# The sample's expert keys moved out of the projection stage into the mixer stage before it

## What is computed

```python
h = rmsnorm(x, norm_mix)
z = h @ w_in                                  # 1024 -> 5888 columns, for all rows
oa = windowed attention; ob = retention       # mixers A and B
x = x + (sigmoid(ga) * (oa @ w_branch_a) + sigmoid(gb) * (ob @ w_branch_b)) @ w_out
h2 = rmsnorm(x, norm_ffn)
q = h2 @ w_q                                  # 1024 -> 2048, 8 heads of 2 x 128
s1, s2 = q halves times 128 sub keys each
top 16 of s1, of s2, then of the 256 sums     # 128 experts for each row
y = sum_k gate_k * gelu(h2 . expert_u[k]) * expert_v[k]
out = rmsnorm(x + y, norm_final)
```

## Time and profile before

| | us |
|---|---|
| median of 3 runs | 4076.27 |
| profiled execution | 4112.39 |
| its span | 4110.5 |
| projection stage, in the profile | 469.2 to 1193.9 |

### The profile page before, as it was taken

How to read it: one execution, slowest core, us unless ns; L and a number is a source line. 1 busy time by engine, 2 the same in 40 slices (tenths; PEclk the granted TensorE clock), 3 DMA queues, 4 the chain that set the end, 5 groups by cost and what they waited for, 6 DMA issues and landing times.

```text
span 4110.5 us, 32129 instructions
## 1 busy us (share of the span) xinstructions
PE 3301.0 (80%) x8957; PEld 1632.7 (40%) x8957; DVE 2452.1 (60%) x4977; ACT 1096.7 (27%) x2938; POOL 1758.0 (43%) x1588
## 2 busy tenths in 40 slices
PE   8775597999966888859779779878878978977776
PEld 5453254555644454424224224323333423422222
DVE  0122068995766777555854864774684585485444
ACT  2102010011113333223333233333333333333322
POOL 1020147774743333124454444444444444445553
PEclk9886897999987898979999999999999999999999
DMA  9898999998998888899999999999999999999998
GB/s 351 295 301 311 340 314 400 386 390 343 373 381 334 317 307 306 305 359 421 421 421 416 416 418 400 421 413 410 419 409 409 422 405 411 419 407 423 422 422 353
DMA packets 303298, 1560.95 MB, mean 380 GB/s; under 512 B 31248, under 2 KB 59152, under 8 KB 179856
## 3 DMA queue, kind: packets, MB, share of 16 engines
q0 software_dynamic: 228096, 1300.34, 79.3%
q1 hardware_dynamic: 60448, 237.77, 15.4%
q10 hardware_dynamic: 14592, 21.10, 1.4%
HBM read 1515.44 MB, written 179.04 MB: 412 GB/s over the span
## 4 chain that ended last, share of the span: by engine, by line
DMA 26%; PE 18%; issue 6%; DVE 4%; ACT 1%; POOL 1%; POOLq 0%; ACTq 0%; DVEq 0%
DMA ring<-uv_d,IXD_p 26%; PE ps L1838 15%; PE ps L1810 3%; DVE ring L1937 2%; ACT dg L1881 1%; POOL ring L2043 1%; ACT GE_p L1875 0%; DVE BP_p L1007 0%; DVE CA_p L1012 0%; DVE BV_p L1002 0%; PE ps L1827 0%; DVE CA_p L1419 0%; DVE DOT_p L1937 0%; DVE II_p L1359 0%; DVE ACC L1918 0%
## 5 line engine op out<-in xcount | busy, mean ns | idle before, releaser
L1838 PE MATMUL ps<-ring,dg 128*128 128x512 f32 x3584 | 1704.1, 614 | 456.5 <-ACT dg L1881 428.2
L2043 POOL DMA_INDIRECT ring<-uv_d,IXD_p x896 | 1081.3, 1207 | 1306.6 <-PE ps L1838 1050.1
L1937 DVE CUSTOM_DVE_ANT_0 ring<-ring,H 128x1024 f32<-128x1024 f32 x896 | 1094.6, 1224 | 888.5 <-DMA ring<-uv_d,IXD_p 866.0
L1838 PEld LDWEIGHTS ps<-ring,dg 128*128 128x128 f32 x3584 | 663.5, 194 | 1415.9 <-issue 717.7
L1260 PE MATMUL ps<-w,xg 128*128 128x368 f32 x1792 | 577.9, 482 | 43.8 <-issue 41.3
L1875 ACT ACTIVATE GE_p<-DOT_p 128x2 f32<-128x2 f32 x448 | 91.1, 203 | 1483.3 <-DVE DOT_p L1937 1483.3
L1260 PEld LDWEIGHTS ps<-w,xg 128*128 128x128 f32 x1792 | 345.6, 193 | 275.7 <-issue 70.2
L1881 ACT ACTIVATE dg<-gdi,GE_p 128x128 f32<-128x128 f32 x896 | 310.7, 394 | 48.3 <-ACT GE_p L1875 3.9
L1869 ACT ACTIVATE gdi<-ident,GD_p 128x128 f32<-128x128 f32 x896 | 303.2, 386 | 25.8 <-issue 19.4
L145 POOL DMA_DIRECT2D uv_d<-in_peer_u x88 | 45.7, 520 | 493.7 <-DMA uv_d<-in_peer_v 283.2
L1289 ACT ACTIVATE zo<-ps,rstd 128x368 f32<-128x368 f32 x112 | 62.6, 567 | 521.7 <-PE ps L1260 284.0
(11 more groups left out here) (412 smaller groups left out, 2877.3 us busy)
## 6 DMA issues: line engine op xcount, KB each, us to landing
uv_d<-in_peer_u POOLq DMA_DIRECT2D x88, 512.0 KB, 5.2
uv_d<-in_peer_v POOLq DMA_DIRECT2D x88, 512.0 KB, 6.3
w<-in_w_in SPq DMA_DIRECT2D x8, 2944.0 KB
w<-in_w_in SPq DMA_DIRECT2D x16, 1472.0 KB
z_d<-zo ACTq DMA_DIRECT2D x16, 1288.0 KB
rows<-in_peer_w_q SPq DMA_DIRECT2D x20, 1024.0 KB
uv_d<-in_peer_u SPq DMA_DIRECT2D x40, 512.0 KB
uv_d<-in_peer_v SPq DMA_DIRECT2D x40, 512.0 KB
```

Of the source, the lines that this page charges most:

```text
L1838: mm = T.matmul(bank(6 + n), dg[:, k % DR, :], ring[:, k % RS, D + n * 512:D + (n + 1) * 512], start=(k == 0), stop=(k == NK - 1))
L1937: V.tensor_tensor_reduce(out=row, in0=row, in1=H2[:], scale=1.0, scalar=0.0, op0=ALU.mult, op1=ALU.add, accum_out=DOT[:, k:k + 1]).then_in ...
L2043: g.indirect_dma_start(ring[:, n % RS, :], None, uv_d, bass.IndirectOffsetOnAxis(ap=IXD[:, n:n + 1], axis=0)).then_inc(s_ring[n % RS], 16)
```

## The change

Block 0's key pass runs in stage 2. `pe_keys` is split into `pe_keys_rows` (the 8 transposes of h2) and the rest. TensorE does the transposes between `pe_mix_transposes` and `pe_output`, and the rest after `pe_output`, behind waits for the query matrix and for the residual add (which has then read the PSUM banks). ScalarE's copies stand behind its work of block 1. SyncE loads `H` and the key tables ahead of `load_branches`. To make room, the query and score tiles are allocated ahead of both stages and some small tiles of the mixer are laid into free places.

In stage 3 TensorE begins with block 1's key pass alone. VectorE begins with block 0's search, whose scores are there; the 8 multiplications of `xg` follow after its third part. Nothing else of stage 3 changes its order; SyncE loads h2 of block 1 first, and no key tables.

```diff
+                    load_rows(sp, 1)
+                    sp.dma_start(H[:], rows(h2_d, 0)).then_inc(c["hld"], 16)
+                    load_keys_tables(sp)
+                    load_branches(sp)
...
                     pe_mix_transposes(pe, 1)
+                    pe_keys_rows(pe, 0)
                     pe_output(pe, 1)
+
+                    pe.wait_ge(s_cw, 16 * (KT + 2))
+                    pe.wait_ge(s["x1"], 2)
+                    pe_keys(pe, 0)
...
                     act_mix(act, 1)
+                    act_keys_rows(act, 0)
                     act_square2(act, 1)
                     act_root2(act, 1)
+                    act_keys_first(act, 0)
+                    act_keys_second(act, 0)
...
-                    sp.dma_start(H[:], rows(h2_d, 0)).then_inc(c["hld"], 16)
+                    sp.dma_start(H[:], rows(h2_d, 1)).then_inc(c["hld"], 16)
                     sp.dma_start(io[:], t["iota16"]).then_inc(s_cw, 16)
-                    load_keys_tables(sp)
...
-                    sp.wait_ge(c["ht"], 1)
-                    sp.dma_start(H[:], rows(h2_d, 1)).then_inc(c["hld"], 16)
...
-                    pe.wait_ge(s_cw, 16 * (KT + 3))
-                    pe_keys(pe, 0)
+                    pe_keys_rows(pe, 1)
                     pe_keys(pe, 1)
...
-                    v.wait_ge(s_xt, 16 + 16 * KT)
-                    for k in range(KT):
-                        V.tensor_scalar(xg[:, k, :], xg[:, k, :], gm[:, k:k + 1], None, ALU.mult).then_inc(s_xg, 1)
                     v.wait_ge(s_cw, 16 * (KT + 3))
                     v.wait_ge(d["nf"], 16)
                     step = Steps(v, s_vstep, STEPS_C)
                     for part in range(PARTS):
+                        if part == GAIN_AT:
+                            v.wait_ge(s_xt, 16 + 16 * KT)
+                            for k in range(KT):
+                                V.tensor_scalar(xg[:, k, :], xg[:, k, :], gm[:, k:k + 1], None, ALU.mult).then_inc(s_xg, 1)
                         dve_keys(part, v, 0, step)
```

More of the change, by code:

```diff
@@ L830, in trunk_kernel @@
         GD1 = sb(mid, "GD1", [P, NK])
[L832 to L895, removed]
@@ L1184, in dve_experts_ahead, with dve_point, _ @@
                     V.scalar_tensor_tensor(ACCA, row, WG[:, k:k + 1], ACCA, ALU.mult, ALU.add).then_inc(d["freed"], 1)
+        early = ctx.enter_context(ExitStack())
+        kt, H, hT, SC = key_buffers(early, "_s")
+        q_ = ctx.enter_context(ExitStack())
+        Q = sb(q_, "Q_s", [P, 16, P])
+        qT = sb(q_, "qT_s", [P, 16, P])
+        with ExitStack() as b_:
+            (zv, gates, X, Pr, atm, oaT, yn, yT, bg, gf, wo, qdT,
+             outd, kdec, sink, sm2) = prompt_buffers(b_, "_e")
+            spare = FREE + VB + HA * 2 * P
+            mx, ngm, es, rs = [rows64[:, spare + HA * i:spare + HA * (i + 1)] for i in range(4)]
+            stats = rows64[:, spare + 4 * HA:spare + 4 * HA + 6 * HB].rearrange("p (h n) -> p h n", h=HB)
+            mv = rows64[:, spare + 64:spare + 64 + 2 * HB].rearrange("p (h n) -> p h n", h=HB)
+            sdv = rows64[:, spare + 96:spare + 96 + HB]
+            intra, into, qaT, qbT, kbT = score_buffers(b_, "_e")
+            wa, wb, zqk, alibi = shared_rows()
+            alibi_c = zv[:, 0].rearrange("p (h n) -> p h n", h=HA)
+            PT, HO = over(Pr, yT)
+            def dve_point(v, blk, j):
+                pass
+            with nc.Block() as block:
+                @block.sync
+                def _(sp):
+                    load_keys_part(sp, 1)
+                    load_values_part(sp, 1)
+                    load_tables(sp)
+                    load_gates(sp, 1)
+                    load_gains(sp)
+                    load_rows(sp, 1)
+                    sp.dma_start(H[:], rows(h2_d, 0)).then_inc(c["hld"], 16)
+                    load_keys_tables(sp)
+                    load_branches(sp)
+                    load_queries(sp, 1, KT)
+                    store_rows(sp, 1)
+                    sp.wait_ge(s["x1st"], 16 * 2)
+                    sp.wait_ge(s["h2st"], 16 * 2)
+                @block.gpsimd
+                def _(g):
+                    g.wait_ge(s_wb, 16 * 5)
+                    g.sem_inc(s_pool, 1)
+                    pool_table(g, TABLE_BS, TABLE_E)
+                @block.tensor
+                def _(pe):
+                    pe_block(pe, 1, 1, False)
+                    pe.wait_ge(s_wb, 16 * 5)
+                    pe_gated_transposes(pe, 1)
+                    pe_branches(pe, 1)
+                    pe_mix_transposes(pe, 1)
+                    pe_keys_rows(pe, 0)
+                    pe_output(pe, 1)
+                    pe.wait_ge(s_cw, 16 * (KT + 2))
+                    pe.wait_ge(s["x1"], 2)
+                    pe_keys(pe, 0)
+                @block.scalar
+                def _(act):
+                    act.sem_inc(c["v1"], 1)
+                    act_block(act, 1, 1, False)
+                    act_gated(act, 1)
+                    act_sigmoids(act, 1)
+                    act_mix(act, 1)
+                    act_keys_rows(act, 0)
+                    act_square2(act, 1)
+                    act_root2(act, 1)
+                    act_keys_first(act, 0)
+                    act_keys_second(act, 0)
+                @block.vector
+                def _(v):
+                    V.memset(kaT[:, 0], 0.0)
+                    V.memset(va[:, 0], 0.0)
+                    V.memset(alibi_c[:], NEG)
+                    V.memset(st[:], 0.0).then_inc(s["stn"], 1)
+                    dve_block(v, 1, 1, False)
+                    v.wait_ge(s_bw, 16 * 6)
+                    dve_gate(v, 1)
+                    dve_biases(v, 1)
+                    dve_merge(v, 1)
+                    dve_residual(v, 1)
+                    dve_norm2(v, 1)
@@ L1265, in _ @@
                 def _(act):
-                    act.sem_inc(c["v1"], 1)
                     act.sem_inc(s_zact, AB)
-                    for blk in range(2):
-                        act_keys_first(act, blk)
-                        act_keys_second(act, blk)
+                    act_keys_rows(act, 1)
+                    act_keys_first(act, 1)
+                    act_keys_second(act, 1)
                     for n in range(WT * PB):
@@ L1327, in _ @@
                     pool_gathers(g, 1, ORDER1, IXD1)
+        early.close()
         PG, PTS = 3, 4
```

38 lines of the change are left out of this document (22 added, 16 removed).

## The result

The kernel after takes 4103.49 us (median of 4 runs, 4102.77 to 4105.83), the kernel before beside it 4075.52: a ratio of 1.0068, with an interval of 1.0050 to 1.0085. That is **28 us slower**, and outside the range of the prediction. The profiled execution of after took 4103.05 us (span 4101.1), an ordinary one.

What follows compares the result with a forecast made beforehand. The DMA engines were taken to bound the projection stage, TensorE's chain a softer second bound. +27.2 (later stage start) + 2.8 (table to first gather) - 31.8 (gathers onward) = -1.8 us: 4076.3 to 4074.5, range 4058 to 4094.

Steps and rivals of the forecast that it cites:

- The keys aren't hidden: Listed with the rivals, no chance given: moved keys run where DMA has nothing to do; already summed as 27.2 us.
- step 1: Key pass in the mixer stage (stage 2): waits for the query matrix until about 455, so the stage ends 27.2 us later.
- step 4: Table and first gather in the projection stage: 26 parts plus 5 us for tile and store; first gather 617.5, 30 us later.
- four signs of being wrong: Query matrix before 450, table under 85 us, GpSimd waiting over 25 us for block 1's places, last store over 15 from 1188.
- I carry the difference over unchanged: In the sum: the profiled execution's 36 us above the median stay, so the -1.8 us applies to the median, giving 4074.5.
- step 5: First gather to the projection stage's end: gelu waits mostly gone, 571 us instead of 602.8, a gain of 31.8 us.
- the crossing: End of the mixer stage, after the scores: about 1 us until the projection stage starts.
- The term for the search: Behind the first gather, where VectorE is nearly full with the search: DMA losses of 9.5 and 5.5 us shrink to 8.
- that for the ends: DMA loss at the start and end of the stretch behind the first gather: 9 us becomes 8.
- The one of the longer table: Projection stage: GpSimd's 92.9 us table stretches beside two more streams; 8 us more gives 4083; chance 0.10.
- waits vanish: Faster rival, behind the first gather: all 54.5 us of gelu waits come off, kernel 4052, halfway 4063; chance 0.23.

Runs made afterwards that it cites:

- the other trace of after: The changed kernel, unchanged, run again beside the kernel before on one more chip: 4104.98 us (4 runs), ratio 1.0062.

## Why the prediction was wrong

**Right, in the changed kernel's own course.** The products started at 452.7 (forecast 455), took 40.2 us to the scores (40.4), and the stage started at 493.2 (496.4), with the DMA engines idle before it, as said. VectorE's first maximum stood 22.8 us into the stage, released by the final gain (23.2). ScalarE's last copy of block 1's scores ended at 540.5 (545). The first gather waited for no places. "The keys aren't hidden" was right too: the later start, 27.2 us in step 1 and 23.1 measured, is the larger part of what was lost. The last store was forecast at 1188.5 and came at 1182.4, but that is in part luck: the first gather came 7.4 us later than forecast (624.9, outside the 26 to 34 us of step 4), and the stretch behind it was 13.6 us shorter. None of the four signs of being wrong showed, since all of them look at the changed kernel alone, and the error was in the kernel before.

**The step that failed: "I carry the difference over unchanged".** The profiled execution of before stood 36 us above the median. I took the excess for something outside the change's reach. It was the very thing that step 5 meant to win: TensorE's stalls (41.3 us in 35 pieces, a total that the page gives and that I had read as ordinary idle time) made the gelu waits of the earlier trace rows, the gap at 1000 to 1040 and a last store 35.9 us later than in an ordinary execution. The prediction had them in hand: of the 457 us to the last gelu it found 61 that were not work, and took them for the kernel's own. In the ordinary execution that stretch is 399 us (561.1 to 959.7), all of it work. The 31.8 us of step 5 are 8.6 between two traces without stalls (4.6 with the other trace of after), which is about the time of the 4.3 MB already moved beside the table (10.4 us at 412 GB/s). Put 8.6 in its place and the forecast's own sum is 27.2 + 2.8 - 8.6 = +21.4, or 4097.7; the median was 4103.5. The rest are the terms below: 4.1 us less for the stage start and 10.6 more from there to the first gather.

**Mis-sized terms.** The stage start is 23.1 to 24.0 us later, not 27.2: the matrix landed 2.3 us earlier than I had it, and the crossing took 0.3 us instead of 1. The table took 108.5 us, not 97.9, where an ordinary execution of before needs 94.6. In its stretch SyncE's queue moved 4.07 MB and ScalarE's 1.32 MB, in that of before 1.11 and 0: 4.3 MB more, for 13.9 us more. I had counted 2.83 MB and taken 5 us. The share of 0.92 to 0.93 was no room for more: it stayed 0.93 while the rate went from 283 to 290 GB/s.

The page "DMA: Bandwidth & Descriptors" of the Trainium skill, section "Queues, rings and completion order", has each engine take turns between the queues that have work. By that rule a tile's packets are served at once and the copies pay. The traces agree that the copies pay in full. In four traces of the kernel before and its variants with some 1.1 MB beside them the 26 parts took 92.3 to 97.9 us, in three of after and its variants with 5.4 MB 107.2 to 108.5; the means, 95.5 and 107.8, are 12.3 us apart, where the 4.3 MB between them take 10.4 at the gathers' 412 GB/s. The 13.9 of the two traces above is within that scatter.

**Step 5's length.** 571 us were forecast from the first gather, 557.4 measured. The term for the search (8 us) and that for the ends (8) weren't there: 700 to 750 and 830 to 870 moved 413 GB/s in after, since the 334 and 355 of the earlier trace rows belonged to that execution and not to VectorE's search, which is in after as well.

**The rivals.** None of the rivals gave 4103 by its mechanism. The one of the longer table had the right place, and 8 us for it on top of the 5 of step 4; with the step that failed mended (4097.7) it would have been in reach. The rival "waits vanish" is what the trace of after shows (557 us from first gather to last store, 548 forecast), and it brought nothing, because in ordinary executions there were no waits to vanish.

**What stays open:** why TensorE stalls in some executions and on some chips (traces on two chips have none in the projection, those on two others 10 to 65 us), and whether the change makes them longer. The chip of the profiled execution of before is not on record. Within the stalls of that execution the DMA share and rate are as full as elsewhere (1.03 and 412 GB/s from 610 to 700); over all traces with stalls they fall around 620 to 725, 780 to 890 and 930 to 1010 us, though not each time in all three.

## What to carry to other kernels

Where the profiled execution is longer than the median by more than the runs scatter, find the rows that make the excess before anything is costed: a wait that exists only in that execution cannot be won back, and here it was the one that the whole gain rested on. Where DMA bounds the stages around it, an edit that lengthens a stage by compute without transfers costs most of the added length, whatever it frees elsewhere (here a start 23 us later, in a change that cost 28); move transfers into the gap with it, or don't move it. A late first gather was cheap here as long as the engines moved other needed bytes meanwhile: count bytes not yet moved and empty microseconds, not marks.

## What the runs showed of the hardware

- TensorE can run single matmuls with gaps of 0.4 to 2.7 us between them for tens of us, with no wait in the profile. In the profiled execution of before the first two gaps (0.42 and 1.66 us, up to 643.7) stood between matmuls of 0.47 us at a granted clock of 1.00 (635 to 643); behind the third, of 2.34 us, they take 0.77, and the granted clock is 0.50 (1.2 GHz) in 650 to 670. In this trace the lower clock follows the stalls. On the chip with 19 runs from 4082 to 4128 us every trace had stalls; on the chips without them, 25 and 19 runs of the same program spread over 17 and 14 us.
- Stretches made mostly of copies from DRAM to DRAM, counted once, moved 279 to 290 GB/s at a share of 0.92 to 0.93, and more traffic beside them only made them longer; gathers, loads and stores moved 403 to 413 at 1.01 to 1.03.
- A tile or store beside such copies is paid by the copies: 4.3 MB cost 12.3 us in the means of four and three traces, or 2.9 us for each MB (9 to 16 us between single traces).
